# The first attention of a two-block transformer: VectorE's order around the softplus of each head, and two convolution projections inside the last pair

## The chip, the cores and the metric

The kernel runs on one core of a Trainium2 chip. The metric is the device time of one execution in microseconds (us). The engines are TensorE (PE), VectorE (DVE), ScalarE (ACT), GpSimd (POOL) and SyncE (SP, which issues the weight loads). They run side by side and meet at semaphores.

## The reference

Two transformer blocks over 512 tokens of width 1024. The part that the change touches is the mixer of the first block: eight heads of stick-breaking attention, and a short gated convolution.

```python
def short_conv(b_gate, c_gate, xin, conv_w):
    v = c_gate * xin
    S = v.shape[1]
    vp = jnp.pad(v, ((0, 0), (CONV_KSIZE - 1, 0), (0, 0)))
    y = conv_w[0] * vp[:, 0:S, :]
    for k in range(1, CONV_KSIZE):
        y = y + conv_w[k] * vp[:, k:k + S, :]
    return b_gate * y

def stick_breaking_attention(q, k, v):
    ...
        z = jnp.einsum('bhqd,bhkd->bhqk', q_blk, k_c) * scale
        sp = jnp.where(valid, jax.nn.softplus(z), 0.0)
        rem = lax.cumsum(sp, axis=3, reverse=True) - sp
        log_a = jax.nn.log_sigmoid(z) - rem
        a = jnp.where(valid, jnp.exp(log_a), 0.0)
        outs.append(jnp.einsum('bhqk,bhkd->bhqd', a, v_c))

def mixer(u, w_mix_in, b_merge, conv_w, w_conv_out, w_attn_out, w_out):
    proj = u @ w_mix_in
    ...
    cb, cc, cx, q, k, v, ga, gb = jnp.split(proj, idx, axis=-1)
    ya = short_conv(cb, cc, cx, conv_w) @ w_conv_out
    o = stick_breaking_attention(heads(q), heads(k), heads(v))
    yb = o @ w_attn_out
    merged = jax.nn.sigmoid(ga + b_merge[0]) * ya + jax.nn.sigmoid(gb + b_merge[1]) * yb
    return merged @ w_out
```

## The kernel before

Activations lie transposed in SBUF (channels on partitions, 512 tokens along a row). Each fp32 product is done as three products of rounded halves: `uh,wh`, `ul,wh` and `uh,wl`. The weights come in chunks of 128 output channels. For each chunk, in the same order on every queue, SP loads `raw` (a ring of four slots), ScalarE writes the rounded `wh` (its `split`), VectorE writes the rest `wl` (its `split`), and TensorE multiplies (`dense`, 24 matmuls of 512 columns). SP loads a chunk once `wl` of the chunk four places before it is written. A `split` in the code works three chunks ahead (`LEAD`) of the place where it stands.

The first attention takes the heads in four pairs. Pairs 0 to 2 run in a hardware loop (`body(p, False)`), pair 3 is written out behind it (`body(pairs - 1, True)`). Each engine has its own queue with its own hand-written order, and waits only where it is told to. For a head `hh` of pair `p` the way is:

- TensorE computes the scores into PSUM (`scores`, L585 to L588);
- ScalarE computes ln(1 + exp(-|z|)) of them in three passes (`log_terms`, the last is L1087);
- VectorE finishes the softplus (`softplus`, L1619), sums it along the keys with four scans (`suffix_sums`, L1628), and subtracts that from the scores (`log_weights`, L1636);
- ScalarE takes the exponential (`probabilities`, L1094, tile `a_pr`), TensorE turns the probabilities (`turn_probs`, ten transposes, L597), ScalarE and VectorE write their two halves (`turned_hi` L1111, `turned_lo` L1655), and TensorE multiplies them with the values (`values`, L612 and L613).

Between these steps TensorE runs the projections of the next pair (`dense` of q, k, v and the convolution's gate b). In the last pair there is no next pair: `next_first` puts the first convolution projection (c of tile 0, `conv_in(0, 0)`) ahead of the first transposes, and `next_second` puts the second one (x of tile 0, `conv_in(0, 1)`) between the second transposes and the second `values`. Between the first transposes and the first `values` there is nothing.

Behind the attention, the convolution has four tiles `m` of 128 channels. For each, TensorE runs two projections, ScalarE copies the first to `sq` (L1299), VectorE multiplies it with the second (`vcv`, L1932), applies three taps (`ycv`, L1935 and L1939) and the gate (L1941), and the two engines write the halves `y1h` and `y1l`. On ScalarE and VectorE this is a loop of two turns with two tiles each. Then `merge` begins; its first matmul waits until the four tiles' `vcv` are written.

Of the kernel before, what the change touches and what calls it, by code (L numbers as in the profile page):

```python
# [24 lines left out]
S = 512  # L25
D = 1024
DT = D // P
# [55 lines left out]
def build(nc, a, out):  # L83
# [3 lines left out]
    with ctx:  # L87
# [391 lines left out]
        def _(pe):  # L479
# [136 lines left out]
            def attention(name, t, kind, pairs, norm, next_first, next_second):  # L616
# [25 lines left out]
                def body(p, last):  # L642
# [15 lines left out]
                    if not last:  # L658
                        dense(c + 1, it, B_DENSE, DT, uh, ul)

                        pe.wait_ge(A_["q_lo"], p + 2)
                    values(t, A_, p, 0)
# [160 lines left out]
            def conv_in(m, x):  # L823

                pe.wait_ge(CV["v"] if x else CV["c"], m + 1)
                dense(AT_["conv1"] + 2 * m + x, 0, 2 * (m % 2) + x, DT, uh, ul)

            attention("att1", t1, 1, 4, 1, lambda: conv_in(0, 0), lambda: conv_in(0, 1))
            for m in range(1, AT):
                conv_in(m, 0)  # L830
                conv_in(m, 1)
# [9 lines left out]
            def z_in(m):  # L841

                pe.wait_ge(G["z"], m + 1)
                dense(AT_["zu"] + m, 0, m % 2, DT, uh, ul)
# [7 lines left out]
            attention("att2", t2, 2, 8, 3, lambda: z_in(0), lambda: z_in(1))  # L852
# [79 lines left out]
        def _(act):  # L932
# [89 lines left out]

            def attention(name, t, kind, pairs):
# [102 lines left out]
                def body(p, last):  # L1126
# [3 lines left out]
                    if kind == 1:  # L1130
                        probabilities(p, 0)
                    if not last:
                        done(nb + 4, it)
                        q_hi()
# [158 lines left out]
            with act.Fori(0, AT // 2) as i:  # L1293
                for r in range(2):
                    split(nb + 2 * r + LEAD, 4 * i)
                    done(nb + 2 * r, 4 * i)

                    act.wait_ge(CV["v"], 2 * i + (r + 1))
                    act.activation(sq[:, r * S:(r + 1) * S], bank(2 * r), ACT.Copy).then_inc(CV["c"], 1)  # L1299
                    split(nb + 2 * r + 1 + LEAD, 4 * i)  # L1300

                    act.wait_ge(CV["y"], 8 * i + (4 * r + 4))
                    act.activation(tile(y1h, 2 * i + r), ycv[:, r * S:(r + 1) * S], ACT.Copy).then_inc(CV["hi"], 1)
# [91 lines left out]
        def _(dve):  # L1395
# [161 lines left out]
            def attention(name, t, kind, pairs):  # L1557
# [141 lines left out]
                def body(p, last):  # L1699
                    it = 4 * p  # L1700
                    if kind == 1:
                        softplus(p, 0)
                        suffix_sums(p, 0)
                        log_weights(p, 0)
                        split(nb + 3 + LEAD, it)
                        softplus(p, 1)
                        suffix_sums(p, 1)
                    else:
                        normalise(p, 0)
                        split(nb + 3 + LEAD, it)  # L1710
                        maxima(p, 1)
                        if not last:
                            forget_row(p, 0)
                            forget_row(p, 1)
                        normalise(p, 1)
# [3 lines left out]
                    if kind == 1:  # L1719
                        log_weights(p, 1)  # L1720
                    if not last:
                        split(nb + 4 + LEAD, it)
# [12 lines left out]
                    if not last:  # L1735
                        v_lo(p + 1)
                        maxima(p + 1, 0)

# [40 lines left out]
                maxima(0, 0)  # L1779
                if kind == 2:  # L1780
                    normal_lo(6)
                    normal_lo(7)
# [141 lines left out]
            with dve.Fori(0, AT // 2) as i:  # L1924
                for r in range(2):
                    v0, y = r * (S + 2), ycv[:, r * S:(r + 1) * S]
                    split(nb + 2 * r + LEAD, 4 * i)
                    split(nb + 2 * r + 1 + LEAD, 4 * i)

                    dve.wait_ge(CV["c"], 2 * i + (r + 3))  # L1930
                    done(nb + 2 * r + 1, 4 * i)
                    dve.tensor_tensor(vcv[:, v0 + 2:v0 + 2 + S], sq[:, r * S:(r + 1) * S], bank(2 * r + 1), ALU.mult).then_inc(CV["v"], 1)  # L1932
                    dve.wait_ge(CV["v"], 2 * i + (r + 3))
                    kw = [cols[:, bass.ds(2 * i + (C_KW + x * AT + r), 1)] for x in range(3)]
                    dve.tensor_scalar(y, vcv[:, v0:v0 + S], kw[0], None, ALU.mult).then_inc(CV["y"], 1)  # L1935
                    for x in (1, 2):

                        dve.wait_ge(CV["y"], 8 * i + (4 * r + x))
                        dve.scalar_tensor_tensor(y, vcv[:, v0 + x:v0 + x + S], kw[x], y, ALU.mult, ALU.add).then_inc(CV["y"], 1)  # L1939
                    dve.wait_ge(CV["y"], 8 * i + (4 * r + 3))  # L1940
                    dve.tensor_tensor(y, y, tile(cb1, 2 * i + r), ALU.mult).then_inc(CV["y"], 1)  # L1941

                    dve.wait_ge(CV["hi"], 2 * i + (r + 1))
                    dve.tensor_tensor(tile(y1l, 2 * i + r), y, tile(y1h, 2 * i + r).bitcast(F32), ALU.subtract).then_inc(CV["lo"], 1)
# [266 lines left out]
```

## Time and profile before

| | us |
|---|---|
| median of 3 runs | 2174.5 |
| lowest, highest | 2169.87, 2179.68 |
| the profiled execution | 2174.65 |
| its span | 2172.8 |
| TensorE busy | 2104.7 |
| VectorE busy | 1303.6 |
| ScalarE busy | 875.9 |

The span is measured from the first to the last instruction of the program. 1.85 us of the profiled execution lie around it. Busy time says how much work an engine has. Where it waits, and for whom, is read from the timeline of the stretch. All times of the trace are counted from the start of the span.

### The profile page before, as it was taken

What the parts mean: (1) busy time and instruction counts of PE and PEld (TensorE: products, weight loads), DVE (VectorE), ACT (ScalarE), POOL (GpSimd) and SP (SyncE); (2) the same over time, 40 slices, a digit from 0 to 9 for tenths busy, and PEclk for the clock granted to TensorE, in tenths of its full rate; (3) what the DMA queues carried; (4) which work ended last, traced back from release to release, by engine and by line L of the source; (5) the groups of instructions that cost most, each with busy time, mean ns of one, the idle gap of its engine ahead of it and who ended that gap; (6) DMA issues with size and microseconds to landing.
All of it is one profiled execution on the core that took longest, in us unless ns stands there. A gap on an engine that the chain in (4) does not pass through costs nothing.

```text
span 2172.8 us, 28697 instructions
## 1 busy us (share of the span) xinstructions
PE 2104.7 (97%) x9448; PEld 1730.1 (80%) x9448; DVE 1303.6 (60%) x1595; ACT 875.9 (40%) x1257; POOL 320.1 (15%) x240
## 2 busy tenths in 40 slices
PE   7999999999999989999999899998999999999998
PEld 5888888777788878888887788877788888888876
DVE  5777676677644453333357777668333577547767
ACT  5322223376433333223235566653322344334444
POOL 2999995000000000000000000012000000000000
PEclk9999999899999989999999999999999999999999
DMA  8666664222233313223323222233333333333222
GB/s 291 186 188 186 196 190 127 80 68 68 57 92 94 110 53 106 87 88 113 92 72 92 75 69 68 59 77 78 102 91 97 95 90 92 88 103 96 77 87 87
DMA packets 372865, 226.29 MB, mean 104 GB/s; under 512 B 8481, under 2 KB 361922, under 8 KB 372816
## 3 DMA queue, kind: packets, MB, share of 16 engines
q1 hardware_dynamic: 362976, 193.49, 30.5%
q0 software_dynamic: 9840, 32.16, 5.4%
q8 instruction: 28, 0.46, 0.1%
q14 instruction: 21, 0.17, 0.0%
HBM read 223.52 MB, written 2.10 MB: 104 GB/s over the span
## 4 chain that ended last, share of the span: by engine, by line
PE 89%; DVE 6%; ACT 2%; issue 2%; DMA 0%; DVEq 0%; SPq 0%; POOL 0%; ACTq 0%
PE ps L482 28%; PE ps L484 28%; PE ps L483 28%; PE ps L597 1%; DVE x L1628 1%; PE ps L574 1%; DVE wl L1401 1%; PE ps L585 1%; PE ps L613 1%; PE ps L612 1%; PE ps L586 1%; DVE x L1619 1%; DMA wada<-in_w_ada 0%; DVE ada_acc L1849 0%; DVE x L1636 0%
## 5 line engine op out<-in xcount | busy, mean ns | idle before, releaser
L482 PE MATMUL ps<-uh,wh 128*128 128x512 f32 x1856 | 732.5, 395 | 10.3 <-DVE ul L1454 4.2
L484 PE MATMUL ps<-uh,wl 128*128 128x512 f32 x1856 | 726.7, 392 | 0.0
L483 PE MATMUL ps<-ul,wh 128*128 128x512 f32 x1856 | 726.5, 391 | 0.0
L1401 DVE TENSOR_TENSOR wl<-raw,wh 128x1024 fp32r<-128x1024 f32 x389 | 547.7, 1411 | 207.0 <-ACT wh L940 200.7
L940 ACT ACTIVATE wh<-raw 128x1024 fp32r<-128x1024 f32 x389 | 408.1, 1052 | 194.3 <-PE ps L484 192.4
L482 PEld LDWEIGHTS ps<-uh,wh 128*128 128x128 f32 x1856 | 351.5, 189 | 83.7 <-issue 11.5
L484 PEld LDWEIGHTS ps<-uh,wl 128*128 128x128 f32 x1856 | 350.7, 189 | 74.3
L483 PEld LDWEIGHTS ps<-ul,wh 128*128 128x128 f32 x1856 | 351.4, 189 | 72.1 <-issue 0.5
L482 PE MATMUL ps<-ah,wh 128*128 128x512 f32 x528 | 208.9, 396 | 0.0
L484 PE MATMUL ps<-ah,wl 128*128 128x512 f32 x528 | 208.8, 396 | 0.0
L483 PE MATMUL ps<-al,wh 128*128 128x512 f32 x528 | 208.8, 395 | 0.0
L1528 DVE TENSOR_TENSOR prod<-sq,ps 128x512 f32<-128x512 f32 x44 | 30.3, 688 | 222.6 <-PE ps L484 216.1
L2144 POOL TENSOR_TENSOR ada_acc<-ada_acc,ada_ring 128x1024 f32<-128x1024 f32 x49 | 141.9, 2895 | 3.8
L1011 ACT ACTIVATE ah<-prod 128x512 f32 x66 | 41.7, 632 | 247.2 <-DVE prod L1528 247.0
L2151 POOL DMA_DIRECT2D nbf<-in_b_f x1 | 0.6, 567 | 810.6 <-DVE h L1484 810.6
L484 PEld LDWEIGHTS ps<-ah,wl 128*128 128x128 f32 x528 | 99.2, 188 | 24.0
L482 PEld LDWEIGHTS ps<-ah,wh 128*128 128x128 f32 x528 | 99.2, 188 | 24.0
L483 PEld LDWEIGHTS ps<-al,wh 128*128 128x128 f32 x528 | 99.2, 188 | 23.9
L1533 DVE TENSOR_TENSOR al<-prod,ah 128x512 f32 x66 | 86.2, 1305 | 20.4 <-ACT ah L1011 20.4
L2140 POOL TENSOR_TENSOR ada_ring<-ada_ring,cact 128x1024 f32<-128x1024 f32 x49 | 96.3, 1965 | 4.1 <-DMA ada_ring<-in_w_ada 3.3
L2185 POOL DMA_DIRECT2D ptok<-in_p x1 | 0.8, 807 | 601.9 <-DVE h L1482 601.9
L950 ACT ACTIVATE sq<-h 128x512 f32 x40 | 25.3, 632 | 140.6 <-DVE h L1484 87.5
(314 smaller groups left out, 2366.5 us busy)
## 6 DMA issues: line engine op xcount, KB each, us to landing
raw<-in_ffn_w_gu SPq DMA_DIRECT2D x88, 512.0 KB, 4.6
raw<-in_w_in SPq DMA_DIRECT2D x57, 512.0 KB, 3.8
ada_ring<-in_w_ada POOLq DMA_DIRECT2D x56, 512.0 KB, 4.1
raw<-in_w_up SPq DMA_DIRECT2D x44, 512.0 KB, 3.8
raw<-in_w_mix_in SPq DMA_DIRECT2D x40, 512.0 KB, 3.8
raw<-in_ffn_w_down SPq DMA_DIRECT2D x32, 384.0 KB, 3.2
raw<-in_ffn_w_down SPq DMA_DIRECT2D x32, 320.0 KB, 3.0
wada<-in_w_ada SPq DMA_DIRECT2D x16, 512.0 KB, 10.1
```

The source lines that it names most:

```text
L482: pe.matmul(dst, lh, rh, start=first, stop=False, skip_group_check=True)
L483: pe.matmul(dst, lh, rl, start=False, stop=False, skip_group_check=True)
L484: return pe.matmul(dst, ll, rh, start=False, stop=last, skip_group_check=True)
L574: x = pe.matmul(bank(5 if v == 5 else 6, v * DT + m, 1), ada_acc[v][:, m * P:(m + 1) * P], one_col[:, :], start=True, stop=True, skip_grou ...
L940: act.activation(wh[:, w], raw[:, w], ACT.Copy).then_inc(w_hi, 1)
L950: act.activation(sq[:, r * S:(r + 1) * S], tile(h, m), ACT.Square).then_inc(sq_done, 1)
L1011: act.activation(tile(ah, 2 * i + r), prod[:, buf], ACT.Copy).then_inc(s_["hi"], 1)
L1401: dve.tensor_tensor(wl[:, w], raw[:, w], wh[:, w].bitcast(F32), ALU.subtract).then_inc(w_lo, 1)
L1528: dve.tensor_tensor(prod[:, buf], factors[0], factors[1], ALU.mult).then_inc(s_["prod"], 1)
L1533: dve.tensor_tensor(tile(al, 2 * i + r), prod[:, buf], tile(ah, 2 * i + r).bitcast(F32), ALU.subtract).then_inc(s_["lo"], 1)
L2140: pool.tensor_tensor(ring[r], ring[r], w, ALU.mult).then_inc(ada_mul, 1)
L2144: pool.tensor_tensor(acc, acc, ring[r], ALU.add).then_inc(ada_add, 1)
```

## The change

In the pairs of the first attention VectorE's `softplus` of a pair's first head is moved from the start of the pair to the end of the pair before it, ahead of the attention output's low half (`o1l`). Its `split` of the third chunk ahead is moved from between the two heads to behind the second `log_weights`.

In the last pair a third hook, `next_middle`, lets TensorE run a projection between the first transposes and the first `values`. The hooks now carry `conv_in(0, 0)`, `conv_in(0, 1)` and `conv_in(1, 0)`. The first two use the same PSUM bank, so ScalarE copies the first result out inside the pair (`conv_copy(0)`), and TensorE waits for that copy. ScalarE and VectorE also split one more weight chunk inside the last pair. The convolution's loop is written out, with the copy at the head of each tile, and with VectorE's second split behind its multiplication.

```diff
@@ TensorE @@
+                    if last and kind == 1:
+                        next_middle()
                     values(t, A_, p, 0)
...
             def conv_in(m, x):
 
                 pe.wait_ge(CV["v"] if x else CV["c"], m + 1)
-                dense(AT_["conv1"] + 2 * m + x, 0, 2 * (m % 2) + x, DT, uh, ul)
-
-            attention("att1", t1, 1, 4, 1, lambda: conv_in(0, 0), lambda: conv_in(0, 1))
-            for m in range(1, AT):
+                if m == 2:
+                    pe.wait_ge(CV["v"], m + 1)
+                if (m, x) == (0, 1):
+                    pe.wait_ge(CV["c"], 2 + 1)
+                dense(AT_["conv1"] + 2 * m + x, 0, 2 * (m % 2) + (x if m else 0), DT, uh, ul)
+
+            attention("att1", t1, 1, 4, 1, lambda: conv_in(0, 0), lambda: conv_in(0, 1), lambda: conv_in(1, 0))
+            conv_in(1, 1)
+            for m in range(2, AT):
                 conv_in(m, 0)
                 conv_in(m, 1)
@@ ScalarE @@
+            def conv_copy(m):
+
+                done(AT_["conv1"] + 2 * m, 0)
+                act.wait_ge(CV["v"], m + 1)
+                act.activation(sq[:, m % 2 * S:(m % 2 + 1) * S], bank(2 * (m % 2)), ACT.Copy).then_inc(CV["c"], 1)
...
                     soft(p, 1)
                     if kind == 1:
                         probabilities(p, 0)
+                        if last:
+                            conv_copy(0)
+                            split(AT_["conv1"] + LEAD, 0)
...
+            for m in range(AT):
+                if m > 0:
+                    conv_copy(m)
+                split(nb + 2 * m + 1 + LEAD, 0)
+                if m < AT - 1:
+                    split(nb + 2 * m + 2 + LEAD, 0)
+
+                act.wait_ge(CV["y"], 4 * m + 4)
+                act.activation(tile(y1h, m), ycv[:, m % 2 * S:(m % 2 + 1) * S], ACT.Copy).then_inc(CV["hi"], 1)
@@ VectorE @@
                     if kind == 1:
-                        softplus(p, 0)
                         suffix_sums(p, 0)
                         log_weights(p, 0)
-                        split(nb + 3 + LEAD, it)
                         softplus(p, 1)
                         suffix_sums(p, 1)
...
                     if kind == 1:
                         log_weights(p, 1)
+                        split(nb + 3 + LEAD, it)
+                        if last:
+                            split(AT_["conv1"] + LEAD, 0)
...
                         maxima(p + 1, 0)
+                        if kind == 1:
+                            softplus(p + 1, 0)
...
+            for m in range(AT):
+                r = m % 2
+                v0, y = r * (S + 2), ycv[:, r * S:(r + 1) * S]
+                split(nb + 2 * m + 1 + LEAD, 0)
+
+                dve.wait_ge(CV["c"], m + 3)
+                done(nb + 2 * m + 1, 0)
+                dve.tensor_tensor(vcv[:, v0 + 2:v0 + 2 + S], sq[:, r * S:(r + 1) * S], bank(2 * r + 1 if m else 0), ALU.mult).then_inc(CV["v"], 1)
+                if m < AT - 1:
+                    split(nb + 2 * m + 2 + LEAD, 0)
```

In VectorE's queue, at the boundary of two pairs, there stands before (the end of the loop's body and the start of pair 3; `x_104` is the tile of log terms, `o1l` the output's low half):

```order
L1740 ISA [waits att1_o_hi]
L1740 TENSOR_TENSOR o1l<-sq,o1h 128x512
L1783 REGISTER_ALU
L1783 COMPARE_AND_BRANCH
L1619 SCALAR_TENSOR_TENSOR x_104<-ps,x_104 128x1280 [waits att1_ln]
L1628 SCALAR_TENSOR_TENSOR x_104<-x_104 128x128 [waits att1_c]
L1628 SCALAR_TENSOR_TENSOR x_104<-x_104 128x256
L1628 SCALAR_TENSOR_TENSOR x_104<-x_104 128x384
L1628 SCALAR_TENSOR_TENSOR x_104<-x_104 128x512
L1636 TENSOR_TENSOR x_104<-ps,x_104 128x1280 [waits att1_c]
L1401 TENSOR_TENSOR wl<-raw,wh 128x1024 [waits w_hi]
L1619 SCALAR_TENSOR_TENSOR x_104<-ps,x_104 128x1280 [waits att1_ln]
```

and in the changed kernel:

```order
L1633 SCALAR_TENSOR_TENSOR x_104<-ps,x_104 128x1280 [waits att1_ln]
L1757 ISA [waits att1_o_hi]
L1757 TENSOR_TENSOR o1l<-sq,o1h 128x512
L1802 REGISTER_ALU
L1802 COMPARE_AND_BRANCH
L1642 SCALAR_TENSOR_TENSOR x_104<-x_104 128x128 [waits att1_c]
L1642 SCALAR_TENSOR_TENSOR x_104<-x_104 128x256
L1642 SCALAR_TENSOR_TENSOR x_104<-x_104 128x384
L1642 SCALAR_TENSOR_TENSOR x_104<-x_104 128x512
L1650 TENSOR_TENSOR x_104<-ps,x_104 128x1280 [waits att1_c]
L1633 SCALAR_TENSOR_TENSOR x_104<-ps,x_104 128x1280 [waits att1_ln]
```

The softplus of the first head has gone ahead of `o1l` and of the branch, and no `wl` stands between the two heads.

In TensorE's queue, in pair 3 behind the first convolution projection (`a_pr` is turned, `a_pth` are the turned probabilities), there stands before:

```order
L597 MATMUL ps<-ident,a_pr 128x128 [waits att1_p]
L597 MATMUL ps<-ident,a_pr 128x128 x9
L612 MATMUL ps<-a_pth,a_vv 128x512 [waits att1_t_lo,att1_o_s]
L613 MATMUL ps<-a_ptl,a_vv 128x512
L612 MATMUL ps<-a_pth,a_vv 128x384 [waits att1_t_lo]
```

and in the changed kernel:

```order
L597 MATMUL ps<-ident,a_pr 128x128 [waits att1_p]
L597 MATMUL ps<-ident,a_pr 128x128 x9
L482 MATMUL ps<-uh,wh 128x512 [waits w_lo,conv1_c,conv1_v]
L483 MATMUL ps<-ul,wh 128x512
L484 MATMUL ps<-uh,wl 128x512
```

A whole projection (24 matmuls, the first three shown) has come between the transposes and the product with the values, and its first matmul waits for ScalarE's copy (`conv1_c`).

In VectorE's queue of the convolution there stands for a tile before (the start of the loop's body):

```order
L1401 TENSOR_TENSOR wl<-raw,wh 128x1024 [waits w_hi]
L1400 REGISTER_ALU
L1401 TENSOR_TENSOR wl<-raw,wh 128x1024 [waits w_hi]
L1930 ISA
L1405 REGISTER_ALU [waits conv1_c]
L1932 TENSOR_TENSOR vcv<-sq,ps 128x512 [waits chunk_done]
L1935 ISA [waits conv1_v]
L1935 TENSOR_SCALAR ycv<-vcv,cols 128x512
L1938 ISA
L1939 ISA [waits conv1_y]
L1939 SCALAR_TENSOR_TENSOR ycv<-vcv,cols,ycv 128x512
```

and in the changed kernel:

```order
L1415 TENSOR_TENSOR wl<-raw,wh 128x1024 [waits w_hi,filled]
L1950 TENSOR_TENSOR vcv<-sq,ps 128x512 [waits chunk_done,conv1_c]
L1415 TENSOR_TENSOR wl<-raw,wh 128x1024 [waits w_hi]
L1955 TENSOR_SCALAR ycv<-vcv,cols 128x512 [waits conv1_v]
L1959 SCALAR_TENSOR_TENSOR ycv<-vcv,cols,ycv 128x512 [waits conv1_y] x2
L1961 TENSOR_TENSOR ycv<-ycv,cb_96 128x512 [waits conv1_y]
L1964 TENSOR_TENSOR y1l<-ycv,y1h 128x512 [waits conv1_hi]
```

The multiplication `vcv` has moved ahead of the second `wl`, and the waits of the loop's form, which are rows of their own (ISA, REGISTER_ALU), have gone into the instructions.

## Rows read from the trace of the kernel before

**Rows 1.** The page's part 4, the chain that ended last, by engine.

```profile
PE 89%; DVE 6%; ACT 2%; issue 2%; DMA 0%; DVEq 0%; SPq 0%; POOL 0%; ACTq 0%
```

**Rows 2.** Waits of TensorE from 400 to 640 us: total us, times, longest.

```profile
PE ps L597 <- ACT a_pr L1094: 7.6, 7, 1.8
PE ps L612 <- DVE a_ptl L1655: 3.6, 1, 3.6
```

**Rows 3.** Timeline of TensorE in pair 1: start, us, instruction, idle time before it.

```profile
487.64 0.39 PE L484 MATMUL ps<-uh,wl 128*128 128x512 f32 x1
488.65 1.31 PE L597 MATMUL ps<-ident,a_pr 128*128 128x128 f32 x10 [0.63 <-ACT a_pr L1094]
489.72 0.48 PE L482 MATMUL ps<-uh,wh 128*128 128x512 f32 x1
...
498.52 1.31 PE L597 MATMUL ps<-ident,a_pr 128*128 128x128 f32 x10 [1.80 <-ACT a_pr L1094]
```

**Rows 4.** Timeline of VectorE in pairs 0 and 1.

```profile
455.00 1.48 DVE L1619 SCALAR_TENSOR_TENSOR x<-ps,x 128x1280 f32<-128x1280 f32 x1
...
480.66 0.69 DVE L1740 TENSOR_TENSOR o1l<-sq,o1h 128x512 f32 x1 [3.73 <-ACT o1h L1164]
481.27 1.48 DVE L1619 SCALAR_TENSOR_TENSOR x<-ps,x 128x1280 f32<-128x1280 f32 x1
482.79 2.97 DVE L1628 TENSOR_TENSOR_SCAN x<-x 128x128 f32<-128x128 f32 x4
...
487.21 1.22 DVE L1401 TENSOR_TENSOR wl<-raw,wh 128x1024 fp32r<-128x1024 f32 x1
488.34 1.48 DVE L1619 SCALAR_TENSOR_TENSOR x<-ps,x 128x1280 f32<-128x1280 f32 x1
```

**Rows 5.** Timeline of ScalarE in pairs 0 and 1.

```profile
453.14 1.37 ACT L1087 ACTIVATE x<-x,one_col 128x1280 f32<-128x1280 f32 x1
...
478.61 1.37 ACT L1087 ACTIVATE x<-x,one_col 128x1280 f32<-128x1280 f32 x1
...
485.13 1.37 ACT L1087 ACTIVATE x<-x,one_col 128x1280 f32<-128x1280 f32 x1
487.32 1.27 ACT L1094 ACTIVATE a_pr<-x 128x1280 f32<-128x1280 f32 x1 [0.83 <-DVE x L1636]
```

**Rows 6.** Timeline of TensorE in pair 3, the convolution and the merge.

```profile
555.30 1.31 PE L597 MATMUL ps<-ident,a_pr 128*128 128x128 f32 x10 [0.61 <-ACT a_pr L1094]
...
572.63 0.39 PE L612 MATMUL ps<-a_pth,a_vv 128*128 128x512 f32 x1
...
573.91 0.40 PE L482 MATMUL ps<-uh,wh 128*128 128x512 f32 x1
...
606.38 0.39 PE L484 MATMUL ps<-uh,wl 128*128 128x512 f32 x1
607.60 0.47 PE L482 MATMUL ps<-uh,wh 128*128 128x512 f32 x1 [0.83 <-issue]
```

**Rows 7.** Two windows: busy us of each engine, then TensorE's granted clock, DMA.

```profile
552.00:577.00 25.00, 19.94 (x86) 16.46 (x85) 14.13 (x20) 9.26 (x14) 0.00 (x0) 0.80 0.08 22
1436.00:1444.00 8.00, 5.96 (x32) 5.38 (x31) 5.09 (x15) 6.06 (x11) 0.41 (x1) 0.79 0.00 0
```

**Rows 8.** Timeline of TensorE in the second window, the one idle stretch.

```profile
1438.65 0.53 PE L612 MATMUL ps<-a_pth,a_vv 128*128 128x512 f32 x1 [2.04 <-DVE a_ptl L1655]
```

**Rows 9.** Timeline of VectorE in the convolution, tile 0 and the start of tile 1.

```profile
577.09 1.23 DVE L1401 TENSOR_TENSOR wl<-raw,wh 128x1024 fp32r<-128x1024 f32 x1 [0.26 <-ACT wh L940]
...
579.76 0.69 DVE L1932 TENSOR_TENSOR vcv<-sq,ps 128x512 f32<-128x512 f32 x1
580.61 0.49 DVE L1935 TENSOR_SCALAR ycv<-vcv,cols 128x512 f32<-128x512 f32 x1 [0.16 <-DVE vcv L1932]
...
585.49 1.23 DVE L1401 TENSOR_TENSOR wl<-raw,wh 128x1024 fp32r<-128x1024 f32 x1 [0.15 <-ACT wh L940]
```

**Rows 10.** DMA issues of the mixer's input weights: count, KB each, us to landing.

```profile
raw<-in_w_mix_in SPq DMA_DIRECT2D x40, 512.0 KB, 3.8
```

More of the change, by code:

```diff
@@ L614, in values, with attention @@
                 mm.then_inc(A_["av"], 1)
-            def attention(name, t, kind, pairs, norm, next_first, next_second):
+            def attention(name, t, kind, pairs, norm, next_first, next_middle, next_second):
                 A_, nb = A[name], AT_[name]
@@ L850, in turn_w @@
                 pe.transpose(bank(4 + m % 2, 0, P), gsm[m % 4][:, 0:P], ident[:, :]).then_inc(G["w_tr"], 1)
-            attention("att2", t2, 2, 8, 3, lambda: z_in(0), lambda: z_in(1))
+            attention("att2", t2, 2, 8, 3, lambda: z_in(0), None, lambda: z_in(1))
             pe.wait_ge(A["att2"]["f_tok"], 1 + 8)
@@ L1292, in _ @@
             nb = AT_["conv1"]
[L1293 to L1303, printed above, removed]
+            for m in range(AT):
[6 more added lines that the diff above has]
+                act.activation(tile(y1h, m), ycv[:, m % 2 * S:(m % 2 + 1) * S], ACT.Copy).then_inc(CV["hi"], 1)
             merge("merge1", m1h, C_BM)
@@ L1779, in attention @@
                 maxima(0, 0)
+                if kind == 1:
+                    softplus(0, 0)
                 if kind == 2:
@@ L1923, in _ @@
             nb = AT_["conv1"]
[L1924 to L1944, printed above, removed]
@@ new lines, in _ @@
+            for m in range(AT):
[7 more added lines that the diff above has]
+                    split(nb + 2 * m + 2 + LEAD, 0)
+                dve.wait_ge(CV["v"], m + 3)
+                kw = [cols[:, C_KW + x * AT + m:C_KW + x * AT + m + 1] for x in range(3)]
+                dve.tensor_scalar(y, vcv[:, v0:v0 + S], kw[0], None, ALU.mult).then_inc(CV["y"], 1)
+                for x in (1, 2):
+                    dve.wait_ge(CV["y"], 4 * m + x)
+                    dve.scalar_tensor_tensor(y, vcv[:, v0 + x:v0 + x + S], kw[x], y, ALU.mult, ALU.add).then_inc(CV["y"], 1)
+                dve.wait_ge(CV["y"], 4 * m + 3)
+                dve.tensor_tensor(y, y, tile(cb1, m), ALU.mult).then_inc(CV["y"], 1)
+                dve.wait_ge(CV["hi"], m + 1)
+                dve.tensor_tensor(tile(y1l, m), y, tile(y1h, m).bitcast(F32), ALU.subtract).then_inc(CV["lo"], 1)
```

## The prediction

> **What bounds the kernel now.** I read the chain that ended last first: TensorE holds 89% of it [rows 1]. So a change here is worth the TensorE idle time that it fills, plus the time lost at half clock, and nothing else. Next I read TensorE's waits around the stretch [rows 2]: seven waits for the probabilities, 7.6 us, and one of 3.6 us for the turned probabilities' low half. Then the timeline, to see what each wait hangs on.
>
> In a middle pair (pair 1; pair 2 repeats it) the last matmul before the first transposes starts at 487.64. A matmul of this size follows the one before it after 0.227 us (24 of them take 5.45 us: six projections from 573.91 to 606.38 + 0.23 = 606.61 [rows 6]). TensorE was therefore free at 487.87 and started at 488.65, when ScalarE's exponential (487.32 + 1.27) was done [rows 3, 5]. The second transposes start at 498.52 behind an idle stretch of 1.80 us. Both wait for a chain on VectorE: softplus, scans, subtraction, one head behind the other.
>
> In pair 3 the stretch from the first transposes (555.30) to the next projection behind the last values (573.91) takes 18.61 us [rows 6]. Its work at full clock is two transposes of 1.07 (489.72 − 488.65 [rows 3]), two products with the values of 1.28 (573.91 − 572.63) and one projection of 5.45, in all 10.15. So 8.46 us are lost. Two idle stretches are in it, the 3.6 us of [rows 2] and a short one, and the granted clock: 0.80 over 25 us, which is 10 us at 1.2 instead of 2.4 GHz [rows 7]. It fell after TensorE had stood idle for most of 3.6 us.
>
> **The change, part by part.**
>
> *Softplus ahead of o1l.* Before, VectorE waits idle for o1h, writes `o1l` at 480.66, the softplus at 481.27, the scans at 482.79 [rows 4]. ScalarE's logarithm ends at 478.61 + 1.37 = 479.98 [rows 5]. The softplus can then start at 480.02, `o1l` at 480.02 + 1.41 = 481.43 (1.49 less the 0.08 by which independent instructions overlap), and the scans at 481.43 + 0.61 = 482.04. That is 0.75 earlier. `o1h` is done before 480.66, so `o1l` waits for nothing, and behind it in VectorE's queue stand only these scans. The exponential ends 0.75 earlier too, at 487.84. TensorE, free at 487.87, starts at 487.92: **0.73 us** gained at the first transposes.
>
> *Split behind the second head.* Before, the second softplus waits for the `wl` at 487.21 and starts at 488.34 [rows 4]. Without it the slot is 486.46, and the logarithm of the second head ends at 485.13 + 1.37 = 486.50 [rows 5]. So it starts at 486.54, 1.80 earlier, and so do the scans, the subtraction and the exponential. The second transposes start **1.78 us** earlier (the 0.73 is in it). The moved split now ends about 1.3 us before TensorE can start the projection that needs it, because both follow the same subtraction: 1.41 and 1.22 us on VectorE against 1.41, 1.27 and 1.07 of subtraction, exponential and transposes. Behind it, the split of the next chunk and the halves of k come at most 0.4 us later against the shifted rest, into idle VectorE time. Pair 0 gains less: its softplus is held by a logarithm that ends at 453.14 + 1.37, so it moves from 455.00 to 454.55, **0.45 us** [rows 4, 5]. Sum over pairs 0, 1 and 2: 0.45 + 2 × 1.78 = 4.01; pair 3's first transposes add 0.73. **4.74 us.**
>
> *The moved load.* SP may load a raw slot only when its `wl` is written. For the moved chunk that is some 8 us later in each pair. The load takes 3.8 us [rows 10]. ScalarE wants the data only at the head of the next pair: pairs follow each other by 488.34 − 455.00 = 33.3 us [rows 4], less the 1.8 gained, and the new release lies about 15 us behind a pair's head, so 16 us remain. Cost nothing; the cover is 12 us. SP's later loads queue behind it, but their own slots come free later still.
>
> *A projection into the hole.* `conv_in(0, 1)` needs ScalarE's copy of the first projection: that one ends at about the moment the first transposes start (+0.2), the copy takes 0.6 and the transposes 1.07. TensorE waits 0 to 0.1 us. The projection then covers 5.45 us. In it VectorE writes the turned halves and the second subtraction, and ScalarE the second exponential; by the shifted rows it ends 0.5 us before TensorE wants it. So no idle stretch above 0.1 us stays in the pair, and nothing is left that took the clock down. Bounds: the copy and the new split make ScalarE 1.6 us busier ahead of the first turned halves, but their path is shorter by the 1.80 above. I take the whole **8.46 us**; with only the idle time filled and the clock down all the same it would be some 5.
>
> *The convolution written out.* TensorE enters it one projection ahead. VectorE does not: it starts when the last output half is written, at 577.09 in the old frame, counted from the last product with the values at 572.63 [rows 6, 9]. Until now it had time to spare. A tile takes it 577.09 to 585.49, 8.40 us. Written out, the second split no longer waits (−0.27), the multiplication's round trip is hidden (−0.16), four waits of 0.16 for its own result shrink to 0.04 (−0.5; 0.04 is what softplus to scans shows: 481.27 + 1.48 to 482.79 [rows 4]), and ScalarE's copy now stands ahead of the first split (+0.45). About 7.9. The fourth `vcv` ends at 577.09 + 3 × 7.9 + 1.15 + 0.69 = 602.6. TensorE is through at 573.91 + 5 × 5.45 = 601.2. It waits 1.4 to 1.5 us before the merge, where it waited 607.60 − 606.61 = 1.0 before. **−0.5 us.** If the waits stay at 0.16, VectorE is 1.5 us later and the term is −2.0; if they vanish it is +1.0, no wait at all.
>
> The Trainium skill ("VectorE: DVE Perf Modes", section on the DRAIN) says of chained VectorE instructions that "the semaphore costs nothing extra here". By that the chain would gain its 4 × 0.12 us per tile more and the merge would wait for nothing, at some 2160.5 us. The trace does not bear it out: an independent instruction starts 0.08 before the end of the one before, a dependent one 0.04 or 0.16 behind it [rows 4, 9].
>
> **The sum.** 4.74 + 8.46 − 0.5 = 12.7 us. Against the profiled execution, 2174.65, that is 2161.95. It lies within 0.2 us of the median of 2174.5. Forecast **2162.0 us**, 0.58% faster. A measurement of this kernel tells about 0.5%, that is 10.9 us, from no change.
>
> **The rivals.**
>
> *The convolution takes it back.* The fill works, but TensorE now stands before the merge for up to 3 us, and the clock falls. For: VectorE becomes the bound there; an idle stretch of 2.04 us [rows 8] stood ahead of a window with the clock at 0.79 over 8 us, 1.7 us of work at full clock [rows 7]. Against: behind the idle 1.80 us the ten transposes took 1.31 us, as behind 0.63 us, so that stretch left the clock alone [rows 3]. Price: 1.5 for the longer wait, 1.7 for the clock, up to 5 if it stays down as long as in pair 3. 2162 + 3.2 = 2165, at most 2168.5. Gain 6 to 9.5 us, within 0.5%. Chance 0.22.
>
> *The fill is held.* The copy stands in ScalarE's in-order queue behind the exponential, and TensorE's projection waits for it; or the clock falls in pair 3 though the idle time is gone, because transposes and short products fill the stretch. Then 3.5 us of the 8.46 are missing: 2165.5. For: ScalarE gets 1.6 us more in the tightest place. Against: the copy's source is done before the transposes end. Chance 0.12.
>
> *Slower: the later release starves the loads.* Place: SP's queue in pairs 0 to 2. If the load of the moved chunk, with those queued behind it, landed later than ScalarE's split at the head of the next pair, every microsecond beyond would shift that pair. It decides at a landing 12 us above the 3.8 of [rows 10]. To eat 12.7 us and another 10.9 it would have to be 20 us above it, in three pairs (3 × 7.9). 2186. Nothing in the profile speaks for it. Chance 0.04.
>
> *The change does nothing in the pairs,* because ScalarE's logarithm, not VectorE, holds each softplus. Pair 0 shows this for the second head (0.45 instead of 1.80). In pairs 1 and 2 the logarithm ends at 486.50, 0.04 from deciding. If it did decide, 1 us would be lost per pair: 2164. Chance 0.07.
>
> *The chained waits cost nothing once written out.* VectorE is through with the fourth `vcv` 1.5 us earlier, TensorE waits for nothing before the merge, the term is +1.0: 2160.5. For: the loop's form had rows of its own for them. Against: softplus to scans has no such row in pair 3 and waits all the same. Chance 0.05. It is the case that the page's sentence above would give.
>
> **How the numbers follow.** The forecast has 0.50, its own range 2159 to 2164.5 (from +1.0 to −2.0 in the convolution, and the clock elsewhere). The range 2157.5 to 2168 takes in the next two rivals. Most of the forecast's 0.50, the 0.05 of the free waits and parts of the rivals at 2164, lie below 2163.6: faster 0.60, same 0.36, slower 0.04.
>
> **What would show it.** In the profile after: no idle stretch before the first transposes of pairs 1 to 3; about 0.7 to 0.9 us instead of 1.80 before the second; a projection between transposes and values in pair 3, with clock 1.00 through it; the second softplus right behind the first subtraction; a tile of the convolution every 7.9 us on VectorE; TensorE's wait before the merge at 1.5 us. I am wrong if the clock falls in pair 3 or at the merge, if VectorE's tile takes over 8.5 us, or if the stretch from 441 us to the merge is shortened by less than 10 us.

## The result and the profile after

The changed kernel took 2163.1 us (median of 7 runs, 2161.1 to 2165.9). The kernel before took 2178.4 us beside it (7 runs, 2169.9 to 2179.7). The ratio over all these runs is 0.994, with a 95% interval of 0.9929 to 0.9951 (the two medians alone give 0.993). The profiled execution took 2161.8 us, with a span of 2159.7 instead of 2172.8. The forecast was 2162.0.

The page of the changed kernel: the chain that ended last, by engine, and from its part 1 the busy times.

```profile
PE 2100.0 (97%) x9448; PEld 1726.3 (80%) x9448; DVE 1288.9 (60%) x1595; ACT 876.8 (41%) x1257; POOL 309.8 (14%) x240
...
PE 91%; DVE 4%; ACT 2%; issue 1%; DMA 1%; SPq 1%; POOL 0%; DVEq 0%; ACTq 0%
```

TensorE holds 91% of the chain, 89% before [rows 1]. It was 2104.7 us busy before, and no matmul was added or removed.

Waits of TensorE in the changed kernel from 400 to 640 us: total us, times, longest. Of the two rows of [rows 2] the first is left, and the wait before the merge is shown below it:

```profile
PE ps L597 <- ACT a_pr L1107: 2.4, 3, 0.8
PE ps L482 <- issue: 1.2, 1, 1.2
```

The seven waits for the probabilities are three, and the wait for `a_ptl` is gone. The timeline of TensorE shows where they stand: the first scores, pair 1 from 487.98, pair 3 from 550.82.

```profile
441.56 0.47 PE L585 MATMUL ps<-a_ka,a_qa 128*128 128x512 f32 x1 [0.78 <-ACT sq L1201]
...
487.98 1.31 PE L597 MATMUL ps<-ident,a_pr 128*128 128x128 f32 x10
496.82 1.31 PE L597 MATMUL ps<-ident,a_pr 128*128 128x128 f32 x10 [0.79 <-ACT a_pr L1107]
...
550.82 0.39 PE L484 MATMUL ps<-uh,wl 128*128 128x512 f32 x1
551.06 1.31 PE L597 MATMUL ps<-ident,a_pr 128*128 128x128 f32 x10
552.13 0.47 PE L482 MATMUL ps<-uh,wh 128*128 128x512 f32 x1
...
557.70 0.39 PE L612 MATMUL ps<-a_pth,a_vv 128*128 128x512 f32 x1
...
558.98 1.25 PE L597 MATMUL ps<-ident,a_pr 128*128 128x128 f32 x10
...
565.55 0.39 PE L612 MATMUL ps<-a_pth,a_vv 128*128 128x512 f32 x1
...
593.86 0.39 PE L484 MATMUL ps<-uh,wl 128*128 128x512 f32 x1
595.48 0.47 PE L482 MATMUL ps<-uh,wh 128*128 128x512 f32 x1 [1.23 <-issue]
```

A row without a bracket started as soon as TensorE was free. The first transposes of the pair have none; before, 0.63 stood there, and 0.79 now stands where 1.80 stood [rows 3]. In pair 3 a projection (552.13) has come between transposes and values, and nothing waits.

One window over pair 3 (columns as in [rows 7]: after the length the busy times, then the granted clock):

```profile
545.00:570.00 25.00, 25.00 (x129) 21.14 (x128) 17.95 (x25) 14.11 (x19) 0.00 (x0) 1.00 0.15 43
```

TensorE is busy for all 25 us, and the clock is 1.00 where it was 0.80.

VectorE's timeline in the changed kernel: the end of pair 0, then tiles 0 and 1 of the convolution.

```profile
480.12 1.49 DVE L1633 SCALAR_TENSOR_TENSOR x<-ps,x 128x1280 f32<-128x1280 f32 x1 [3.08 <-ACT x L1100]
481.52 0.68 DVE L1757 TENSOR_TENSOR o1l<-sq,o1h 128x512 f32 x1
482.12 2.97 DVE L1642 TENSOR_TENSOR_SCAN x<-x 128x128 f32<-128x128 f32 x4
485.12 1.49 DVE L1650 TENSOR_TENSOR x<-ps,x 128x1280 f32<-128x1280 f32 x1
486.63 1.49 DVE L1633 SCALAR_TENSOR_TENSOR x<-ps,x 128x1280 f32<-128x1280 f32 x1
...
570.06 1.23 DVE L1415 TENSOR_TENSOR wl<-raw,wh 128x1024 fp32r<-128x1024 f32 x1 [0.31 <-ACT wh L947]
571.32 0.69 DVE L1950 TENSOR_TENSOR vcv<-sq,ps 128x512 f32<-128x512 f32 x1
571.92 1.22 DVE L1415 TENSOR_TENSOR wl<-raw,wh 128x1024 fp32r<-128x1024 f32 x1
573.05 0.48 DVE L1955 TENSOR_SCALAR ycv<-vcv,cols 128x512 f32<-128x512 f32 x1
573.57 1.54 DVE L1959 SCALAR_TENSOR_TENSOR ycv<-vcv,cols,ycv 128x512 f32<-128x512 f32 x2
...
577.97 1.23 DVE L1415 TENSOR_TENSOR wl<-raw,wh 128x1024 fp32r<-128x1024 f32 x1 [0.74 <-ACT wh L947]
```

The softplus now stands ahead of `o1l`, and the second head's softplus starts 0.02 us behind the subtraction, with no `wl` between. A tile takes 577.97 − 570.06 = 7.91 us (8.40 before [rows 9]). The dependent tap starts 0.04 behind its predecessor's end (573.05 + 0.48 to 573.57), where a wait in a row of its own cost 0.16.

**The measure used below.** The stretch from the first scores (L585) to the merge's first matmul (L482) holds everything that the change touches. Before it is 607.60 − 441.02 = 166.58 us, after 595.48 − 441.56 = 153.92: **12.66 us shorter**. It is read within one profile, where a ratio's interval is 4 to 6 us wide. Between two profiles of one kernel it agrees to 0.02 us as long as TensorE's clock does not fall (the changed kernel: 153.92, and 153.90 in a0_changed below); where the clock falls, it moved by 1.4 us (b1_before_again below). So each comparison below says what the clock did. Before and behind the stretch the two spans differ by 0.4 us: 13.1 in all.

### The profile page after: what moved, and what is told of

It reads as the page before. It is cut to its first block, busy times and chain, and to the rows that moved or that the text cites. A ratio compares the mean times of both kernels' runs of the same rounds, so it can differ in the third digit from the quotient of the medians.

```text
span 2159.7 us, 28626 instructions
## 1 busy us (share of the span) xinstructions
PE 2100.0 (97%) x9448; PEld 1726.3 (80%) x9448; DVE 1288.9 (60%) x1595; ACT 876.8 (41%) x1257; POOL 309.8 (14%) x240
## 4 chain that ended last, share of the span: by engine, by line
PE 91%; DVE 4%; ACT 2%; issue 1%; DMA 1%; SPq 1%; POOL 0%; DVEq 0%; ACTq 0%
PE ps L482 29%; PE ps L484 28%; PE ps L483 28%; PE ps L597 1%; PE ps L585 1%; PE ps L574 1%; PE ps L586 1%; PE ps L613 1%; PE ps L612 1%; DVE wl L1415 0%; PE ps L813 0%; DMA wada<-in_w_ada 0%; PE ps L588 0%; SPq L380 0%; DMA xtok<-in_x 0%
## 5 line engine op out<-in xcount | busy, mean ns | idle before, releaser
L482 PE MATMUL ps<-uh,wh 128*128 128x512 f32 x1856 | 733.2, 395 | 11.1 <-issue 4.3
L484 PE MATMUL ps<-uh,wl 128*128 128x512 f32 x1856 | 726.9, 392 | 0.0
L1415 DVE TENSOR_TENSOR wl<-raw,wh 128x1024 fp32r<-128x1024 f32 x389 | 539.1, 1390 | 212.2 <-ACT wh L947 205.8
L482 PEld LDWEIGHTS ps<-uh,wh 128*128 128x128 f32 x1856 | 351.5, 189 | 84.5 <-issue 12.3
L484 PEld LDWEIGHTS ps<-uh,wl 128*128 128x128 f32 x1856 | 350.8, 189 | 74.5
L482 PE MATMUL ps<-ah,wh 128*128 128x512 f32 x528 | 208.9, 396 | 0.0
L484 PE MATMUL ps<-ah,wl 128*128 128x512 f32 x528 | 208.8, 396 | 0.0
L2164 POOL TENSOR_TENSOR ada_acc<-ada_acc,ada_ring 128x1024 f32<-128x1024 f32 x49 | 129.8, 2648 | 3.8
L484 PEld LDWEIGHTS ps<-ah,wl 128*128 128x128 f32 x528 | 99.2, 188 | 24.0
L482 PEld LDWEIGHTS ps<-ah,wh 128*128 128x128 f32 x528 | 99.2, 188 | 24.0
L1014 ACT ACTIVATE sq<-ps 128x512 f32<-128x512 f32 x44 | 26.4, 599 | 139.1 <-PE ps L484 139.1
```

The lines of the kernel that those rows point to most:

```text
L482: pe.matmul(dst, lh, rh, start=first, stop=False, skip_group_check=True)
L484: return pe.matmul(dst, ll, rh, start=False, stop=last, skip_group_check=True)
L1014: act.activation(sq[:, buf], bank(2 * r), ACT.Silu).then_inc(s_["gate"], 1)
L1415: dve.tensor_tensor(wl[:, w], raw[:, w], wh[:, w].bitcast(F32), ALU.subtract).then_inc(w_lo, 1)
L2164: pool.tensor_tensor(acc, acc, ring[r], ALU.add).then_inc(ada_add, 1)
```

## The experiments

**e1_order** moves the softplus and the split, and nothing else. **e2_conv** is the changed kernel without these two: the projection in pair 3, the copy inside the pair, and the written-out loop.

```diff
(e1_order, against the kernel before)
-                        softplus(p, 0)
                         suffix_sums(p, 0)
                         log_weights(p, 0)
-                        split(nb + 3 + LEAD, it)
...
                         log_weights(p, 1)
+                        split(nb + 3 + LEAD, it)
...
                         maxima(p + 1, 0)
+                        if kind == 1:
+                            softplus(p + 1, 0)
```

> The kernel before with the two moves in VectorE's queue alone (softplus of a pair's first head ahead of o1l, the split behind the second subtraction); hooks, bank use and convolution loop as before. Theory (TensorE waits for VectorE's chain, the terms add up): 4.0 us over pairs 0 to 2, the second transposes of pair 3 another 1.8 us earlier, the idle stretch before the first values of pair 3 shrinks from 3.6 to about 2.5 us; 5.8 us faster if the clock falls there all the same, 8.2 us if it does not. Rival (the whole gain comes from the filled hole and the clock, ScalarE's logarithm holds the pairs): within 1 us of before.

> The changed kernel with VectorE's order in the pairs put back (softplus at the head of the pair, split between the two heads); the projection in the hole and the written-out convolution stay. Theory: pairs 0 to 2 as before; in pair 3 an idle stretch of about 0.6 us before the first transposes and 0.6 us before the second, none before the values, clock at full; merge wait 1.4 us. 7.3 us faster than before. Rival (the fill is held by ScalarE's copy, or the clock falls anyway): 2 to 4 us faster. Rival (everything comes from here): 12.7 us faster.

Measured, in the stretch: e1_order −5.50 us (603.02 − 441.94 = 161.08) where 5.8 was expected, ratio 0.9971 (0.9961 to 0.9982); e2_conv −7.31 us (601.63 − 442.36 = 159.27) where 7.3 was expected, ratio 0.9968 (0.9956 to 0.998). Timeline of TensorE and a window in e1_order:

```profile
555.27 0.47 PE L612 MATMUL ps<-a_pth,a_vv 128*128 128x512 f32 x1 [2.57 <-DVE a_ptl L1655]
...
558.81 2.39 PE L597 MATMUL ps<-ident,a_pr 128*128 128x128 f32 x10 [1.95 <-ACT a_pr L1094]
...
549.00:574.00 25.00, 20.48 (x93) 16.85 (x92) 14.63 (x21) 10.59 (x15) 0.00 (x0) 0.86 0.08 22
```

The hole of pair 3 is smaller (2.57 instead of 3.6 [rows 2]) but the clock still falls: 0.86 over 25 us, and ten transposes take 2.39 instead of 1.31. The first transposes of pair 3 stand at 551.39, 109.45 us behind the first scores and so 4.83 earlier than before; pair 3 gave only 0.7 of the 5.50. In e2_conv:

```profile
556.63 1.31 PE L597 MATMUL ps<-ident,a_pr 128*128 128x128 f32 x10 [0.61 <-ACT a_pr L1107]
565.08 1.31 PE L597 MATMUL ps<-ident,a_pr 128*128 128x128 f32 x10 [0.40 <-ACT a_pr L1107]
...
550.00:575.00 25.00, 23.99 (x122) 20.03 (x122) 17.75 (x22) 12.64 (x17) 0.00 (x0) 1.00 0.15 43
```

The projection fills the hole and the clock stays at 1.00, without the softplus's help. The two parts add: 5.50 + 7.31 = 12.81 against 12.66 together. So neither part does the work alone. That they add this closely is in part chance: in pair 3 e1_order gained 0.7, and how much it gains there hangs on where the clock is down; e2_conv fell 0.6 short of the changed kernel there (16.35 us from the first transposes to the projection behind the last values, against 15.77), because its second transposes still wait.

**e4_softplus** moves the softplus alone, **e5_split** the split alone.

```diff
(e5_split, against the kernel before)
                         log_weights(p, 0)
-                        split(nb + 3 + LEAD, it)
                         softplus(p, 1)
...
                         log_weights(p, 1)
+                        split(nb + 3 + LEAD, it)
```

> The kernel before with only the softplus of the first head moved ahead of o1l. Theory: everything behind it on VectorE 0.75 us earlier in pairs 1, 2 and 3, nothing in pair 0; first transposes of these pairs wait for nothing, the second ones wait as long as before: 2.2 us faster, the clock still falls in pair 3. Rival (o1l, not the softplus, was what mattered and it now comes late): no gain or slower.

> The kernel before with only the split moved behind the second subtraction. Theory: the second softplus 0.45 us earlier in pair 0 and 1.13 us in pairs 1 to 3, first transposes wait as before: 3.8 us faster (0.45 + 3 x 1.13), clock in pair 3 still falls. Rival (the weight half comes late for the projection that needs it, or the load behind it does): TensorE waits for wl in the pairs, no gain.

e5_split: −4.80 us (602.88 − 441.10 = 161.78), ratio 0.9981 (0.9971 to 0.999). Up to the second transposes of pair 3 it gained the expected 3.8 us (559.99 − 441.10 = 118.89 against 122.73 before). The 1 us more came behind them, where the clock came back earlier: it was down for 6.8 us in pair 3 instead of 10.2. e4_softplus missed: −0.21 us (606.41 − 440.04 = 166.37), ratio 0.9994 (0.9984 to 1.0004). Up to the second transposes of pair 2 it did what it should: 529.30 − 440.04 = 89.26 against 90.81 before, −1.55. Then came this (timeline of TensorE and a window in e4_softplus):

```profile
529.30 1.50 PE L597 MATMUL ps<-ident,a_pr 128*128 128x128 f32 x10 [1.79 <-ACT a_pr L1094]
...
558.52 0.77 PE L612 MATMUL ps<-a_pth,a_vv 128*128 128x512 f32 x1 [3.59 <-DVE a_ptl L1655]
...
525.00:540.00 15.00, 13.21 (x64) 11.15 (x63) 9.48 (x13) 7.38 (x11) 0.00 (x0) 0.89 0.24 70
```

Behind an idle stretch of 1.79 us the clock was down for 3.4 us in pair 2 (0.89 over 15 us). The kernel before has an idle stretch of the same length there, and its profile showed 1.00. Was this e4's doing, or chance?

**e4b_softplus_again** is the same kernel, profiled once more. **b1_before_again** is the kernel before, profiled once more. Each is a single profiled execution.

> The kernel with only the softplus moved, a second profile. In the first one the clock fell for 3.4 us behind the idle 1.79 us of pair 2, which the same idle time had not done before. If that was chance of the moment, the fall is absent here and the stretch to the merge is some 1.7 us shorter (about 164.5 us against 166.4); if it belongs to this order, it is there again.

> The kernel before, a second profile. If a fall of the clock behind an idle 1.80 us is chance, it may show here in pair 1 or 2, with a stretch from the first scores to the merge of some 168 us; otherwise the stretch takes 166.6 us again.

In e4b the clock fell again, in the same place (behind 1.78 us; the stretch 166.21). So it did in the kernel before, with nothing changed. Two windows over pairs 2 and 3 and TensorE's timeline in b1_before_again:

```profile
525.00:540.00 15.00, 13.20 (x59) 11.08 (x58) 12.96 (x18) 8.35 (x14) 0.00 (x0) 0.89 0.34 99
562.00:572.00 10.00, 7.05 (x27) 5.95 (x28) 6.01 (x9) 3.33 (x5) 0.00 (x0) 0.66 0.00 0
...
533.42 2.19 PE L597 MATMUL ps<-ident,a_pr 128*128 128x128 f32 x10 [1.80 <-ACT a_pr L1094]
535.26 0.77 PE L482 MATMUL ps<-uh,wh 128*128 128x512 f32 x1
```

and the same window in the first profile of the kernel before:

```profile
525.00:540.00 15.00, 13.20 (x69) 11.15 (x68) 11.38 (x16) 8.05 (x13) 0.00 (x0) 1.00 0.25 72
```

The same program, the same idle 1.80 us, the same 13.20 us busy: clock 1.00 in one execution and 0.89 in the other, where a matmul of 512 columns takes 0.77 us instead of 0.39. The stretch is 610.57 − 442.59 = 167.98 in b1, 1.40 longer than in the first profile. The fall in pair 2 cost 1.65 us: the first transposes of pair 3 stand at 558.52 − 442.59 = 115.93 instead of 555.30 − 441.02 = 114.28. In pair 3 the clock of b1 was down for 6.8 us instead of 10.2, and that gave only 0.25 back. Second transposes of pair 3, in the first profile of before and in b1:

```profile
563.75 2.39 PE L597 MATMUL ps<-ident,a_pr 128*128 128x128 f32 x10 [0.85 <-ACT a_pr L1094]
...
566.96 2.39 PE L597 MATMUL ps<-ident,a_pr 128*128 128x128 f32 x10 [1.53 <-ACT a_pr L1094]
```

Most of the 3.4 us that b1 was spared lay ahead of these transposes, in the idle hole and in the first products with the values; TensorE then only waited longer for the probabilities, 1.53 instead of 0.85. What a fall costs in pair 3 is decided behind the second transposes. From there to the projection behind the last values TensorE needs 7.85 us at full clock (566.83 − 558.98). It took 10.16 in the first profile of before, 9.92 in b1, 10.66 in e4, 10.53 in e1 and 9.20 in e5, each above it by about half the time that the clock was still down behind the transposes (4.7, 4.2, 5.9, 5.6 and 2.9 us).

So compare e4_softplus with b1, whose clock fell in the same place of pair 2. The second transposes of pair 3 stand at 562.06 − 440.04 = 122.02 in e4 (122.05 in e4b) and at 566.96 − 442.59 = 124.37 in b1: 2.35 us earlier, where 2.2 was expected. The softplus gained what it should. The miss is the fall in pair 2, 1.65 us, and a later return of the clock in pair 3, 0.5 us. Behind an idle stretch of 1.8 us the clock falls in some executions and not in others. Whether the moved softplus makes a fall more likely, two profiles of it can't tell.

**e9_hole_empty** takes the projection out of the hole again and puts it behind the attention; copy, splits and written-out loop stay. It asks whether the written-out loop brings anything by itself.

```diff
(e9_hole_empty, against the changed kernel)
-                    if last and kind == 1:
-                        next_middle()
                     values(t, A_, p, 0)
...
-            attention("att1", t1, 1, 4, 1, lambda: conv_in(0, 0), lambda: conv_in(0, 1), lambda: conv_in(1, 0))
+            attention("att1", t1, 1, 4, 1, lambda: conv_in(0, 0), None, lambda: conv_in(0, 1))
+            conv_in(1, 0)
             conv_in(1, 1)
```

> The changed kernel with the hole of pair 3 left empty: c of tile 0 ahead of the first transposes, x of tile 0 behind the second ones, c of tile 1 behind the attention; VectorE's order in the pairs and the written-out convolution stay. Theory (the filled hole brings the gain, writing the loop out brings none): as with the two moves in VectorE's queue alone, the stretch from the first scores to the merge takes about 161 us, 5.5 us less than before, with idle stretches of some 2.6 and 2 us and a fallen clock in pair 3. Rival (the written-out convolution brings a part of its own): under 160 us.

Measured: −6.21 us (600.89 − 440.52 = 160.37, about 161 was expected), ratio 0.9966 (0.9956 to 0.9977). TensorE in e9_hole_empty:

```profile
553.88 0.47 PE L612 MATMUL ps<-a_pth,a_vv 128*128 128x512 f32 x1 [2.57 <-DVE a_ptl L1668]
...
557.42 2.40 PE L597 MATMUL ps<-ident,a_pr 128*128 128x128 f32 x10 [1.17 <-ACT a_pr L1106]
```

The idle 2.57 us of e1_order is back, and the fallen clock with it (down for 6.8 us). The projection in the hole is worth 12.66 − 6.21 = 6.45 us on top of the moved order. The 0.7 us that e9 has over e1_order are no gain of copy, splits or written-out loop, but of where the clock was down. The second transposes of pair 3 stand at the same place in both (557.42 − 440.52 = 116.90 and 558.81 − 441.94 = 116.87). Behind them TensorE takes 9.71 us to the projection behind the last values instead of 10.53: behind these transposes the clock stays down for another 3.8 us in e9 and 5.6 in e1. In narrow windows it falls in e9 at 554.4, while the products with the values run, and in e1 at 557.5, behind them. So these products ended later in e9, and the wait behind them is shorter (1.17 instead of 1.95). From there to the merge both take the same (33.76 and 33.68 us), as the kernel before does (33.69).

**e6_last_tile** and **e7_weights_first** go for what the change leaves: a wait of 1.39 us before the merge, and 2.40 us of idle time before the second transposes of pairs 0 to 2. **e8_both** has both edits.

```diff
(e6_last_tile, against the changed kernel)
-                split(nb + 2 * m + 1 + LEAD, 0)
+                if m < AT - 1:
+                    split(nb + 2 * m + 1 + LEAD, 0)
...
-                if m < AT - 1:
-                    split(nb + 2 * m + 2 + LEAD, 0)
+                split(nb + 2 * m + (2 if m < AT - 1 else 1) + LEAD, 0)
```

```diff
(e7_weights_first, against the changed kernel: ahead of turned_lo instead of behind it)
                         suffix_sums(p, 1)
+                        log_weights(p, 1)
...
                     if kind == 1:
-                        log_weights(p, 1)
                         split(nb + 3 + LEAD, it)
```

> The changed kernel with the split of the convolution's last tile put behind that tile's multiplication. Theory (VectorE's queue is what TensorE waits for before the merge): the fourth vcv comes 1.14 us earlier, the wait before the merge shrinks from 1.4 us to about 0.25, 1.1 us faster than the changed kernel. Rival (that wait is TensorE's own, since the profile calls it issue): no change.

> The changed kernel with the second head's subtraction put ahead of the low half of q and of the turned low halves, in all four pairs. Theory (VectorE's chain to the second exponential is what is left of the wait): the subtraction comes 2.9 us earlier, no idle stretch before the second transposes (now 0.8 us idle, 0.95 us lost, three times), but 0.1 to 0.2 us before the first values: 2.3 us faster than the changed kernel. Rival (the turned low halves, now 1.4 us later, take it back): no change or slower.

> The last two edits together. Theory: they add up, 3.4 us faster than the changed kernel, some 16 us faster than before. Rival: the convolution's VectorE queue eats it; the wait before the merge grows by what the pairs gain.

> The changed kernel once more, as the base of the three kernels that go with it: 12.7 us faster than before by the theory, 13 by its first profile. The clock falls in no stretch between 441 us and the merge.

Against the changed kernel's 153.92, e6 is 0.37 us shorter (594.76 − 441.21), e7 1.93 (594.14 − 442.15), e8 2.26 (593.55 − 441.89). The two edits add up (0.37 + 1.93 = 2.30), but to less than the expected 3.4. a0_changed, the changed kernel again, came to 153.90, and neither in it nor in e6, e7 or e8 did the clock fall in the stretch (1.00). The ratios to the kernel before are 0.9935 (0.9922 to 0.9949) for e6 and for e7 (0.9921 to 0.9949), 0.9922 (0.9908 to 0.9936) for e8, and 0.9942 (0.9929 to 0.9956) for a0. Timeline of VectorE and TensorE at the merge in e6_last_tile:

```profile
593.48 0.39 PE L484 MATMUL ps<-uh,wl 128*128 128x512 f32 x1
593.97 0.69 DVE L1951 TENSOR_TENSOR vcv<-sq,ps 128x512 f32<-128x512 f32 x1 [1.55 <-PE ps L484]
594.76 0.47 PE L482 MATMUL ps<-uh,wh 128*128 128x512 f32 x1 [0.90 <-issue]
```

With the split out of its way VectorE now stands idle for 1.55 us and waits for the projection. The fourth `vcv` reads that projection's result, which is done at 593.48 + 0.39 = 593.87. It then takes 0.10 + 0.69 us, and the merge starts 0.10 later. Counted from TensorE being free (593.48 + 0.23) that is 1.05 us, about the wait of before. The expected 1.1 us was wrong; only 0.37 is to be had while the merge waits for this `vcv`. VectorE's timeline in the kernel before shows the same hand-over:

```profile
606.81 0.69 DVE L1932 TENSOR_TENSOR vcv<-sq,ps 128x512 f32<-128x512 f32 x1 [2.12 <-PE ps L484]
```

There too VectorE stood idle, for 2.12 us, until the last projection was done, and the merge followed at 607.60, 0.10 behind the `vcv`. So the wait of 1.0 us before was already all hand-over. The e7 edit removed the waits before the second transposes of pairs 0 to 2 that I had aimed at (465.29, 496.19 and 527.10 stand without a bracket), and gave 1.93 of the expected 2.3. e8_both is the fastest kernel here, 2159.8 us by its median; its interval and the changed kernel's overlap, so only the stretch shows that it is faster.

## Why the prediction was right

The time, 2163.1, lies 1.1 us from the forecast, and the mechanism is the one it named. That the time itself came so close is in part luck: the forecast took the kernel before as 2174.65, and beside the changed kernel it took 2178.4. The shortening of the stretch, 12.66 for 12.7, is the better witness. By its own terms, the stretch being cut at the first transposes of pair 3 and at the projection behind the last values:

| term | forecast | measured | how |
|---|---|---|---|
| pairs 0 to 2, first transposes of pair 3 | 4.74 | 4.78 | (555.30 − 441.02) − (551.06 − 441.56) |
| hole of pair 3 filled, clock kept | 8.46 | 8.29 | lost 8.46 before; after (566.83 − 551.06) − 15.60 = 0.17 |
| convolution and merge wait | −0.5 | −0.4 | wait 1.0 before; 595.48 − 594.09 = 1.39 after |
| sum | 12.7 | 12.66 | |

The last values start at 565.55, so the next projection stands at 566.83. The 15.60 are the forecast's 10.15 with a second projection of 5.45. The last `L484` at 593.86 leaves TensorE free at 594.09.

- **Pairs.** No idle before the first transposes, 0.76 to 0.85 before the second: as forecast (0.7 to 0.9). e1_order shows that the order of VectorE's queue alone does this.
- **The moved load.** No row of TensorE, ScalarE or VectorE between 400 and 640 us names a DMA as what ended its wait. The rival in which the later release starves the loads fell.
- **The hole.** ScalarE's copy was done before the transposes were. Timeline of ScalarE in pair 3 of the changed kernel:

```profile
551.25 0.60 ACT L1034 ACTIVATE sq<-ps 128x512 f32<-128x512 f32 x1 [0.24 <-PE ps L484]
```

It ends at 551.85, TensorE wants it at 552.13. The rival "the fill is held" fell, with e2_conv's clock of 1.00 as the second witness. In all six profiles with a projection in the hole the clock stays at 1.00 in pair 3 (the changed kernel, a0, e2, e6, e7, e8); in all seven without one it falls.
- **The convolution.** A tile takes 7.91 us for a forecast of 7.9, a dependent tap waits 0.04, and the merge 1.39 for 1.4 to 1.5. This is half a microsecond given back, not the 3 of the rival "takes it back", and no clock fell there. The Trainium skill ("VectorE: DVE Perf Modes", section on the DRAIN) says of chained VectorE instructions that the semaphore "costs nothing extra here". The trace differs from it by 0.13 us a step (a dependent row starts 0.04 behind the end, an independent one 0.09 before it: 573.05 + 0.48 to 573.57, 571.32 + 0.69 to 571.92), and the merge's wait did not go, as the rival by that rule had it. e6_last_tile and the row 606.81 of the kernel before show that even a faster VectorE could have taken that wait only down to about 1.0: the "+1.0, no wait at all" that the prediction gave as the term's best end was out of reach, since the fourth `vcv` has to read TensorE's last projection. That bound was mis-stated, and with it the 2160.5 of the rival "cost nothing once written out", which counts on it; the forecast itself does not use it.
- **What was wrong in the argument.** Against the rival "takes it back" I wrote that the idle stretch of 1.80 us "left the clock alone". One profile carried that. In three of four later profiles with such a stretch in pair 2 (e4_softplus, e4b, b1; not e2_conv) the clock fell behind it, and in pair 1 in none. The conclusion held for the changed kernel, whose idle stretch before the merge is 1.23 us by the same bracket (1.39 counted from TensorE being free); the argument does not hold as a rule. Nor did the clock fall after "most of 3.6 us" of idle time in pair 3, as I wrote: in narrow windows over that profile it is down from 558.3, 1.7 us into the stretch (555.30 + 1.31 = 556.61). This bears on the size as well: later medians of the kernel before were 2175 to 2178. That would fit executions in which pair 2 loses 1.7 us too; the runs that were timed leave no trace, so this part of the 15 us between the medians is argued, not shown.

## What to carry to other kernels

When TensorE is the bound, add up an idle stretch and what the clock takes behind it. Of the clock count only what is slowed behind the last wait: 3.4 us less at half clock gave 0.25 us back where a wait stood behind them, and about half their length where none did. Moving an independent projection into one hole was worth 6.45 us here, shortening the waits of all four pairs by reordering 5.5. Ask of a wait at a stage's end what it must read last: the merge waited for a product with TensorE's own last result, so with VectorE idle and waiting for it 1.0 us was still left. And put an edit's effect on a stretch between two named instructions inside one profile: there 0.4 us can be read, where the timed runs leave an interval of 4 to 6 us. But say beside it what the clock did, and take a second profile of the kernel before: without b1 the 0.2 us of e4_softplus would have passed for what its edit is worth.

## What the runs showed of the hardware that was not expected

In pair 2 an idle stretch of 1.8 us of TensorE (1.78 to 1.81) was followed by the clock at 1.2 GHz for 3.4 us in three profiles (b1_before_again, e4_softplus, e4b_softplus_again: 0.89 over 15 us) and by 2.4 GHz throughout in two (the first profile of before with 1.80, e2_conv with 1.81: 1.00). One program showed both. Behind the same 1.79 to 1.80 us in pair 1 the clock stayed at 1.00 in all five. At the larger hole of pair 3 (2.46 to 3.60 us) it fell in every profile that had it, for 10.2 us in three (before, e4_softplus, e4b) and for 6.8 us in four (b1, e1_order, e5_split, e9_hole_empty). Where it fell differed: inside the hole in before, e4, e4b and e5, 0.5 to 2.2 us behind its end in b1, e1 and e9. The Trainium skill ("TensorE: Matmul & The Clock Gate", section on why this matters for your kernels) ties the drop to idle gaps longer than this one. The rows here differ from it in three of ten cases, and the measurement decides: in these three, 1.8 us were enough. What decides between two executions of one program stays open.
